# Two-layer diffusion backbone: token blocks over the last two down pieces, and modulation pieces loaded into freed activation space

## The reference, cut to what matters

```python
def _ada(cond, w, b):
    m = (jax.nn.silu(cond) @ w + b)[:, None, :]
    return jnp.split(m, N_MOD, axis=-1)          # N_MOD = 6, w is 1024 x 6144 a layer

def _swiglu(h, wg, wu, wd):
    return (jax.nn.silu(h @ wg) * (h @ wu)) @ wd   # 1024 -> 2816 -> 1024

for i in range(DEPTH):                             # layer 0 even, layer 1 odd
    ...
    x = x + g1 * _rms_norm(y, norm_g[1])
    h2 = _modulate(_rms_norm(x, norm_g[2]), sh2, sc2)
    x = x + g2 * _rms_norm(ffn(h2), norm_g[3])
    if need_ctx:
        ...
        ctx = ctx + cg2 * _rms_norm(ffn(hc2), norm_g[3])
```

## Time and profile before

| | |
|---|---|
| three runs | 1632.62, 1635.84 (median), 1636.05 us |
| profiled execution | 1637.03 us, span of its instructions 1635.4 us |
| mean granted clock of TensorE | 0.992 |
| TensorE busy | 1596.7 us, 98% of the span |
| DVE, ACT, POOL busy | 69%, 57%, 3% |
| read from memory | 404 MB, 262 GB/s over the span |

### The profile page before, as it was taken

The page is one execution under the profiler, slowest core; times in us unless marked ns, Lnnn a source line. Parts: engine busy times, 40 slices in busy tenths (PEclk is TensorE's granted clock), DMA queues, the critical chain, the costliest instruction groups (busy, mean ns, idle before and its releaser), DMA issues.

```text
span 1635.4 us, 22633 instructions
## 1 busy us (share of the span) xinstructions
PE 1596.7 (98%) x8278; PEld 1299.9 (79%) x8278; DVE 1126.2 (69%) x1482; ACT 930.8 (57%) x1343; POOL 50.2 (3%) x70
## 2 busy tenths in 40 slices
PE   7999999999999999899999999999999999999997
PEld 3886588988888888689687888888888888888885
DVE  5444433657653333643768999998999999899997
ACT  4415433622222322632667787787778777777875
POOL 0000000400000000000101000000000000000010
PEclk9999999999999999999999999999999999999998
DMA  8622732797442322642257999999999999999982
GB/s 345 218 77 103 309 119 84 263 366 249 159 178 96 111 103 103 234 144 78 65 205 280 420 420 421 380 391 374 389 378 368 388 357 415 358 398 367 381 332 64
DMA packets 68730, 428.88 MB, mean 262 GB/s; under 512 B 8880, under 2 KB 12720, under 8 KB 20656
## 3 DMA queue, kind: packets, MB, share of 16 engines
q1 hardware_dynamic: 60000, 396.93, 63.1%
q0 software_dynamic: 8656, 30.96, 5.1%
HBM read 404.25 MB, written 23.61 MB: 262 GB/s over the span
## 4 chain that ended last, share of the span: by engine, by line
PE 92%; DVE 4%; ACT 2%; DMA 1%; issue 1%; SPq 0%; DVEq 0%; ACTq 0%
PE ps L2052 28%; PE ps L2054 28%; PE ps L2053 28%; PE ps L2116 2%; DMA raw<-in_w 1%; PE ps L2070 1%; PE ps L2629 1%; DVE small L1465 1%; PE ps L2292 1%; PE ps L2313 1%; DVE raw L1693 1%; DVE raw L1692 0%; PE ps L2591 0%; PE ps L2281 0%; PE ps L2317 0%
## 5 line engine op out<-in xcount | busy, mean ns | idle before, releaser
L1865 DVE TENSOR_TENSOR wl<-raw,wh 128x1024 fp32r<-128x1024 f32 x522 | 615.5, 1222 | 59.2 <-ACT wh L1112 52.3
L1112 ACT ACTIVATE wh<-raw 128x1024 fp32r<-128x1024 f32 x522 | 524.9, 1057 | 93.2 <-PE ps L2054 93.2
L2052 PE MATMUL ps<-wh,ah 128*128 128x512 f32 (+1 forms) x864 | 330.0, 382 | 0.8 <-DVE al L1704 0.3
L2054 PE MATMUL ps<-wh,al 128*128 128x512 f32 (+1 forms) x864 | 320.9, 371 | 0.0
L2053 PE MATMUL ps<-wl,ah 128*128 128x512 f32 (+1 forms) x864 | 320.2, 371 | 0.0
L2052 PE MATMUL ps<-ah,wh 128*128 128x512 f32 (+1 forms) x802 | 290.7, 362 | 3.7 <-DVE al L1328 1.5
L2054 PE MATMUL ps<-ah,wl 128*128 128x512 f32 (+1 forms) x802 | 282.9, 353 | 0.0
L2053 PE MATMUL ps<-al,wh 128*128 128x512 f32 (+1 forms) x802 | 282.8, 353 | 0.0
L2052 PE MATMUL ps<-wh,sh 128*128 128x512 f32 x536 | 210.2, 392 | 1.5 <-DVE sl L1570 1.5
L2054 PE MATMUL ps<-wh,sl 128*128 128x512 f32 x536 | 209.4, 391 | 0.0
L2053 PE MATMUL ps<-wl,sh 128*128 128x512 f32 x536 | 208.8, 390 | 0.0
(11 more groups left out here) (315 smaller groups left out, 1220.9 us busy)
## 6 DMA issues: line engine op xcount, KB each, us to landing
raw<-in_w SPq DMA_DIRECT2D x372, 1024.0 KB, 7.0
sent<-raw POOLq DMA_DIRECT2D x16, 512.0 KB, 24.6
back<-raw POOLq DMA_DIRECT2D x16, 512.0 KB, 25.4
x<-sent POOLq DMA_DIRECT2D x7, 512.0 KB, 11.5
back<-x POOLq DMA_DIRECT2D x7, 512.0 KB, 8.6
x<-in_x SPq DMA_DIRECT2D x2, 1024.0 KB, 8.9
raw<-in_ukv SPq DMA_DIRECT2D x1, 1024.0 KB, 7.2
ah<-flat_rows POOLq DMA_DIRECT2D x2, 512.0 KB, 5.4
```

The costliest lines, as they stand in the source:

```text
L1112: act.activation(wh[:, J % SPLITS, piece_half(h)], slot(J % SLOTS)[:, piece_half(h)], ACT.Copy).then_inc(w_hi, 1)
L1865: ins = dve.tensor_tensor(wl[:, J % SPLITS, piece_half(h)], slot(J % SLOTS)[:, piece_half(h)], wh[:, J % SPLITS, piece_half(h)].bitcast(F3 ...
L2052: pe.matmul(out, lh, rh, start=start, stop=False)
L2054: return pe.matmul(out, ll, rh, start=False, stop=stop)
```

## The change

1. *Order of loads.* Modulation pieces 40 to 43 are loaded one by one behind down pieces 6, 7, 8 and 9, and 44 to 47 together behind in-projection piece 3. The list becomes: down 6, mod 40, down 7, mod 41, down 8, mod 42, down 9, mod 43, down 10, in-projection 0 to 3, mod 44 to 47, in-projection 4 and so on.
2. *Slots.* They go into slots that held `hid`: mod 40, 41, 42, 43 into 4, 5, 6, 3, then mod 44, 45, 46, 47 into 4, 5, 6, 4. Each of the first four waits on SP until the chunks of its slot are split: 8, 12, 16 and 4 of them. Main pieces have slots 0, 1, 2 for themselves.
3. *Late chunks.* Chunks 20 and 21 are split into `ah` and `al`, free by then, and wait for no earlier chunk.
4. *Token blocks.* The last four chunks, not two, are taken by token blocks, behind one wait for the split of down piece 10 and for the low parts of all 22 chunks. Down piece 9 counts as used inside the last block.
5. *Turns.* Turn pairs 0 and 1 move into the last token block, ahead of its chunk 20.
6. *Modulation pieces on TensorE.* 40 to 43 stand ahead of chunks 3 to 6 of in-projection 0, and 44 behind it, ahead of 45.
7. *Splits.* The loop of ACT and DVE ends with d = 9. In-projection 1 is split behind the turned chunks: on ACT ahead of the squares of block 3, on DVE behind its gating. On ACT the row copy `rows(10)` moves behind these squares.

```diff
+GAP_FIRST, GAP_SLOTS = 6, (3, 4, 5, 6)
...
-            + main(M_GU + MADE_FIRST + 2 + GAP_MODS - OUT_MODS, M_OIN + 2)
-            + mods(GAP_MODS, GAP_MODS + 5) + main(M_OIN + 2, M_OIN + 3) + mods(GAP_MODS + 5, GAP_MODS + 6) + main(M_OIN + 3, M_OIN + 4)
-            + mods(GAP_MODS + 6, N_MOD) + main(M_OIN + 4, MAIN))
+            + main(M_GU + MADE_FIRST + 2 + GAP_MODS - OUT_MODS, M_DOWN + GAP_FIRST)
+            + [e for i in range(len(GAP_SLOTS)) for e in main(M_DOWN + GAP_FIRST + i, M_DOWN + GAP_FIRST + i + 1) + mods(GAP_MODS + i, GAP_MODS + i + 1)]
+            + main(M_DOWN + GAP_FIRST + len(GAP_SLOTS), M_OIN + 4) + mods(GAP_MODS + len(GAP_SLOTS), N_MOD) + main(M_OIN + 4, MAIN))
...
+        if e[0] == "mod" and e[1] >= GAP_MODS:
+            allowed = GAP_SLOTS if e[1] < GAP_MODS + len(GAP_SLOTS) else GAP_SLOTS[1:]
...
+        late = NF - 2
+        hid_hi = lambda f: sh[:, f % 2, :] if f < late else ah[:, f - late, :]
+        hid_lo = lambda f: sl[:, f % 2, :] if f < late else al[:, f - late, :]
...
+                if kind == "mod" and GAP_MODS <= i < GAP_MODS + len(GAP_SLOTS):
+                    sp.wait_ge(sem("hid_lo"), 4 * (RING_SLOT[p] - EARLY_SLOTS + 1))
...
             def hidden_hi(f):
-                if f >= 2:
+                if 2 <= f < late:
...
-                act.activation(sh[:, f % 2, :], hid[:, f, :], ACT.Copy).then_inc(sem("hid_hi"), 1)
+                act.activation(hid_hi(f), hid[:, f, :], ACT.Copy).then_inc(sem("hid_hi"), 1)
...
-            for d in range(NF // 2):
+            for d in range(NF // 2 - 1):
...
+            split(M_OIN + 1)
+            row_square("y", 3)
             rows(10)
-            row_square("y", 3)
...
-            for d in range(NF // 2):
+            for d in range(NF // 2 - 1):
...
             gated_rows(3)
+            split(M_OIN + 1)
...
-            for f in range(NF - 2):
+            for f in range(NF - 4):
...
             pe.wait_ge(w_lo, M_DOWN + NF // 2)
             pe.wait_ge(sem("hid_lo"), NF)
-            for t in range(ROW_BLOCKS):
-                for f in (NF - 2, NF - 1):
-                    mm = down_rows(f, t)
-                mm.then_inc(sem("y2_ps") if t < ROW_BLOCKS - 1 else w_used, 1)
...
+            for t in range(ROW_BLOCKS):
+                for f in range(NF - 4, NF):
+                    if (t, f) == (ROW_BLOCKS - 1, NF - 2):
+                        pe.wait_ge(sem("tok_made"), 2)
+                        for j in range(2):
+                            turn_pair(N_O1L, j)
+                    mm = down_rows(f, t)
+                    if (t, f) == (ROW_BLOCKS - 1, NF - 3):
+                        mm.then_inc(w_used, 1)
+                mm.then_inc(sem("y2_ps") if t < ROW_BLOCKS - 1 else w_used, 1)
             pe.wait_ge(sem("row_sq"), 2)
             pe.wait_ge(sem("y2_gated"), 2)
-            mod_piece(GAP_MODS)
-            pe.wait_ge(sem("tok_made"), 2)
-            for j in range(2):
-                turn_pair(N_O1L, j)
-            mod_piece(GAP_MODS + 1)
...
-                if k in (3, 4, 5):
-                    filler(GAP_MODS + k - 1)
+                if 3 <= k < 7:
+                    mod_piece(GAP_MODS + k - 3)
...
+                if p == 0:
+                    mod_piece(GAP_MODS + 4)
```

More of the change, by code:

```diff
@@ L1569, in hidden_lo @@
                 dve.wait_ge(sem("hid_hi"), f + 1)
-                dve.tensor_tensor(sl[:, f % 2, :], hid[:, f, :], sh[:, f % 2, :].bitcast(F32), ALU.subtract
+                dve.tensor_tensor(hid_lo(f), hid[:, f, :], hid_hi(f).bitcast(F32), ALU.subtract
                                   ).then_inc(sem("hid_lo"), 1)
@@ L2400, in down_rows @@
                     at = (f % 2) * D + c * 512
-                    mm = mm3(ps[:, ROW_BANKS[t] + c, :], sh[:, f % 2, t * P:(t + 1) * P], sl[:, f % 2, t * P:(t + 1) * P],
+                    mm = mm3(ps[:, ROW_BANKS[t] + c, :], hid_hi(f)[:, t * P:(t + 1) * P], hid_lo(f)[:, t * P:(t + 1) * P],
                              wh[:, b % SPLITS, at:at + 512], wl[:, b % SPLITS, at:at + 512], f == 0, f == NF - 1)
                 return mm
-            for f in range(NF - 2):
+            for f in range(NF - 4):
                 if f % 2 == 0:
```

## The result

| kernel | runs | median us | ratio to before, 95% interval |
|---|---|---|---|
| before | 5 | 1635.84 | |
| changed, first session | 5 | 1643.13 | 1.0044 (1.0030 to 1.0058) |
| changed, second session | 5 | 1642.92 | 1.0042 (1.0028 to 1.0056) |
| changed, third session | 7 | 1642.33 | 1.0045 (1.0031 to 1.0059) |

The change costs 0.42 to 0.45%, some 7 us. The forecast was 1637.6 us, +0.1%, and the range ended at 1641.5. Where a text says how many us less a variant takes than the change, it is the difference of the medians from the 1643.13 of the first session, which is good to some 3 us. One profiled execution of the kernel before, 1780.84 us at a mean granted clock of 0.848, was slow throughout and is left out.

What follows compares the result with a forecast made beforehand. TensorE bounds the kernel, busy 98% of the span. Work of 43.0 us plus waits of 5.4 and 2.1 came to 0.3 us less than before; plus 2.0 us of clock, +1.7 us: 1637.6 us, range 1632.5 to 1641.5.

Steps and rivals of the forecast that it cites:

- one fall of the clock: Behind the new wait at chunk 18: lower clock costs 2.0 us, bounded between nothing and 3.4 us.
- The wait for down piece 9: Before chunk 16: its load, queued behind modulation piece 42's new wait, lands at 630.8, so TensorE stands 2.1 us.
- the stage behind in-projection piece 3: Everything after in-projection piece 3: nothing the change touches, so the difference goes through to the end, no added cost.
- a split ahead of the late chunks: Before chunk 18: in-projection piece 0's split precedes chunks 20 and 21, so TensorE stands 5.4 us waiting for all four chunks.
- The long wait and the fall at the modulation pieces: Around 681 to 691 us: 3.0 us load wait and 3.4 us lost to half clock both go, 6.4 us.
- rival 1: New waits do not appear and the change does all it could: -7.7 us, 1628.1 us; chance 0.13.
- (a): Before the last down piece: 1.5 us TensorE wait on shared hidden buffers goes, as chunks 20 and 21 get their own.
- The sum of the work: From chunk 17 done to modulation piece 46: 43.0 us of work without waits, against 50.7 us before.
- the cover of down piece 8: Down projection: its load lands at about 609, wanted at 611.8; no cost, nearer load's cover given as 2.3 us.
- No wait at piece 45: Modulation pieces after in-projection piece 0: piece 45's load lands about 1 us before its use, so no wait.
- the short stretch: Low clock stretch at 858.3 to 861.8, 3.5 us long, 1.7 us lost; used to choose the clock cost.
- rival 3: Matmuls of chunks 18 to 20: clock takes more, 1639.0 with one full fall, 1642.4 with two; chance 0.20.

Runs made afterwards that it cites:

- The loads alone, well placed: Kernel before with only the new load order, slots and SP waits, modulation pieces 40 to 43 one down piece later: 1631.05 us, ratio 0.9962.
- All three edits together: Changed kernel with modulation loads one down piece later, chunks 20 and 21 split before 18 and 19, modulation piece 45 behind in-projection piece 1: 1629.19 us.
- the wait for each chunk: Kernel with modulation loads later, chunks reordered and piece 45 moved, plus separate TensorE waits for chunks 18 and 19: 1629.04 us, ratio 0.9959.
- the third experiment: Changed kernel with only the split of in-projection piece 0 moved behind chunks 20 and 21 on ACT and DVE, chunk order kept: 1639.48 us.
- The zero matmuls: Changed kernel with three matmuls of zeros in the wait before chunk 16 and five in that before chunk 18: 1639.34 us, ratio 1.0017.
- piece 45 later: Changed kernel with modulation piece 45 and its columns taken behind in-projection piece 1, load order the same: 1641.74 us, ratio 1.0038.

## Why the prediction was wrong, point by point

**The step that failed.** The forecast took one fall of the clock into its sum, 2.0 us. The change has two waits, of which the longer one goes with a fall every time and the shorter one in five profiles of seven, and the runs show about 4 us of clock. Two terms failed beside it. The wait for down piece 9 was put at 2.1 us and measured 3.3, and the stage behind in-projection piece 3, put at nothing, took 0.9 to 2.5 us more. The two mechanisms that were named, a split ahead of the late chunks and a load behind a new wait, are the right ones.

**What bounds the kernel, and what the change removes: right for the loads, wrong for the 1.5 us.** The long wait and the fall at the modulation pieces go, in two of the three profiles of the change. The loads alone, well placed, win 5.7 us of the 6.4 counted. All three edits together give 1629.2, beside the 1628.1 of rival 1, in which no new wait appears. The wait (a) of 1.5 us does not go with the new buffers of chunks 20 and 21. Chunk 19 still waits for chunk 17, and in the kernel with all three edits TensorE stands 1.5 us in front of chunk 18. Only the wait for each chunk removes it in the trace.

**The sum of the work: right.** From the high part of chunk 15 to modulation piece 46 the steps of the prediction make 21.8 + 43.0 = 64.8 us without any wait. The timeline of the kernel with a wait for each chunk, which has no wait of TensorE left, shows it: ACT's high part of chunk 15 and TensorE's piece 46 lie 64.6 us apart. Two small slips change nothing: 43.0 + 5.4 + 2.1 is 50.5 and not 50.4, and from 609 to 611.8 the cover of down piece 8 is 2.8 us and not 2.3.

```profile
618.88 0.63 ACT L861 ACTIVATE sh<-raw 128x512 fp32r<-128x512 f32 x1 [4.81 <-PE ps L2067]
...
683.44 1.07 PE L2129 MATMUL ps<-raw 128*32 128x256 f32 x16
```

**The wait for all four chunks: right to 0.1 us.** 5.36 us in every profile that has it, against 5.4, with the split of in-projection piece 0 as the larger part of it, as the third experiment shows.

**The wait behind the modulation load: right in kind, too small by 1.2 us.** 3.3 us and not 2.1. Down piece 9 was put 2.5 us behind modulation piece 42 by the spacing inside a burst, 7.3 us after the issue of piece 42. It landed 8.6 us after it, 8.2 after its own issue, in the first profile of the change (line of the load: duration of the issuing instruction, start; then issue to landing):

```profile
L555 SPq DMA_DIRECT2D raw<-in_w x1: 432/432/432, 620.7 to 620.7; - x1
...
DMA to landing us min/median/max: 8.2/8.2/8.2
```

In that burst the queues carried one instruction packet as well, of 16 KB; a pair of loads one piece earlier, at 598.6, had none and landed after 4.7 and 6.8 us. All twelve profiles with the new load order have such a packet at this place, and the second load took 8.1 to 8.3 us in each. No run took the packet away, so that it is the cause is argued and not shown. The loads queued behind the pair are not the cause. The burst at 837 in the kernel before has nine loads, not ten. Its second had seven behind it and no packet beside it, and landed after 6.9 us:

```profile
L560 SPq DMA_DIRECT2D raw<-in_w x2: 328/380/432, 837.2 to 837.5; - x2
DMA to landing us min/median/max: 4.8/5.8/6.9
```

The 7.2 us of the earlier trace rows, for one load under a busy queue, would have come nearer by only 0.3 us.

**No wait at piece 45: nearly right.** The prediction has its load landing 7.3 us after the issue of piece 44 (4.8 + 2.5). It landed 10.3, 8.5 and 8.7 us after it in the three profiles, so the cover of about 1 us was not there: waits of 0.3 and 0.5 us in two of them, 2.0 and a fall in the first. The load itself took 6.6 to 8.4 us, and the earlier trace rows, with 7.2, had shown that it could.

**The clock: the step that failed most.** The forecast gave it 2.0 us in all, from a bound of one fall. The zero matmuls show 3.8 to 4.4. The mistake was in two places. The 5.4 us wait goes with 6.8 us at the 1.2 GHz level in all five profiles. The fall begins before the wait ends, and 3.5 to 6.2 us of it lie over dense matmuls in the three profiles of the change, a loss of 1.7 to 3.1 us, while the forecast took a value near the 1.7 us of the short stretch. And the 3.3 us wait brings a fall of its own in five of seven profiles, which the forecast had only inside rival 3. That rival had the mechanism, two falls behind two waits, and its upper point of 1642.4 is where the time lay; it got a chance of 0.20 and the range stopped at 1641.5.

The Trainium skill says in "TensorE: Matmul & The Clock Gate", section "HAM oscillation — how this bites in real kernels", that in a kernel whose groups of matmuls are separated by long waits the clock's cost is paid at each of them again. The runs agree that one fall does not use up the next: both later profiles of the change have two. Which waits are long enough is a matter of this case's rows, and the 3.3 us one was charged in five profiles of seven.

**The routing stage: not in the forecast.** Its low stretch was 3.4 us long in the kernel before, and 10.2, 10.2 and 6.8 in the three profiles of the change. Half of the difference is 1.7 to 3.4 us of lost matmul time; the stage itself took 0.9 to 2.5 us more. The prediction's sentence that behind piece 3 nothing is touched, so that the difference goes through, gave this no term. The variant with only the split behind shows 10.2, those with piece 45 later and with the waits filled 6.8, and the six others 3.4, all with the same program in that stage. Whether an earlier wait moves this, or chance does, stays open.

**The account.** Forecast +1.7 us. Then +1.2 for down piece 9, +1.8 to 2.4 for the clock behind both waits (3.8 to 4.4 less 2.0), +0.3 to 0.5 for piece 45 and +0.9 to 2.5 in the routing stage: +5.9 to +8.3, where the ratios give +6.9 to +7.4 (0.42 to 0.45% of 1636). The terms are enough for what was measured, but several are uncertain by 1 us or more, and the clock behind the waits and the routing stage may be counted in part twice, so their sum is no proof that nothing else plays a part. The kernel with all three edits leaves no room for a large cost of another kind.

## What to carry to other kernels

A wait put into an in-order list of loads delays every later load in the list, and the engine that splits the next of them stands in front of all that its program holds behind it: list what is queued behind the wait, and put the wait where the next load has a whole piece of cover. Where two waits of 3 us and more appear on the engine that sets the time, price the clock behind each of them: here it added about 4 us to 8.7 us of idle time. Moving what is ready ahead of what is not (here chunks 20 and 21 ahead of 18 and 19, and the split for the next stage behind both) turned a loss of 0.44% into a ratio of 0.9990, and with the loads one piece later and piece 45 moved into a gain of 0.42%, with the same work. Run each part of a bundle alone as well: here the loads by themselves, one piece later, gave 0.38%, and what the token blocks add to that is not shown.

## What was not expected of the hardware

**How the clock answers to idle time.** By the length of TensorE's wait between dense matmuls: 1.5 us, no fall in five profiles (before and four experiments); 2.7 us, a fall in the one profile that has it, 3.4 us long; 3.3 us, a fall in five of seven, 3.4 us or more; 5.4 us, a fall of 6.8 us in five of five. So in these profiles the wait of 3.3 us had either outcome, in the same program too (the three of the change), and the wait of 5.4 us only one.

**What keeps it up.** Eight matmuls of zeros in the two waits left the granted clock at 1.00 in both and behind both, as the rows above show, and gave back about half of the change's loss (3.8 to 4.4 of some 7 us).

**One execution is not the rule for a load.** The load of modulation piece 45 took from 6.6 to 8.4 us in the same program, and a single profile made a wait of 2.0 us out of it that two further ones showed as 0.3 and 0.5.
